# Two weight panels loaded during the second attention, and the first token gather of the expert layer in two parts

## The reference

```python
h = rmsnorm(x, attn_norm)
c_q, c_kv, k_r, q_b, k_b, v_b, gate_a, gate_b = split(h @ w_in)
o_a = mla_attention(c_q, c_kv, k_r, q_norm, w_uq, kv_norm, w_ukv, cos_mla, sin_mla)
o_b = moba_attention(q_b, k_b, v_b, cos_moba, sin_moba)
mixed = sigmoid(gate_a) * (o_a @ w_o_mla) + sigmoid(gate_b) * (o_b @ w_o_moba)
x = x + mixed @ w_out
# hierarchical_moe(rmsnorm(x, ffn_norm)):
#   a group of 8 experts by argmax, then the top 2 of the group by softmax;
#   for each expert e and its tokens xb:
#       y = (silu(xb @ w_g[e]) * (xb @ w_u[e])) @ w_d[e]      # 1024 -> 256 -> 1024
#   and the weighted y are added to x
return rmsnorm(x, final_norm)
```

## Time and profile before

| | |
|---|---|
| median of three runs | 698.22 us (697.89 to 699.25) |
| the profiled execution | 697.33 us, of which the span of the trace is 695.5 us |
| mean granted TensorE clock | 0.988 of full speed |
| PE busy | 653.9 us (94%) |
| DVE / ACT / POOL busy | 334.8 / 327.0 / 378.6 us |
| read from HBM | 179.73 MB, 260 GB/s over the span |

### The profile page before, as it was taken

One profiled execution on the slowest core, in us unless ns is written; L12 is line 12 of the kernel. 1 busy time (PEld: TensorE's weight loads), 2 busy tenths in 40 slices (PEclk: granted clock), 3 DMA queues, 4 the chain that ended last, 5 costly groups with the idle time before them and its releaser, 6 DMA issues.

```text
span 695.5 us, 13827 instructions
## 1 busy us (share of the span) xinstructions
PE 653.9 (94%) x5608; PEld 544.4 (78%) x5608; DVE 334.8 (48%) x684; ACT 327.0 (47%) x603; POOL 378.6 (54%) x284
## 2 busy tenths in 40 slices
PE   5999999999999999999999999999999999787894
PEld 4899899999999999998898999999654554343442
DVE  5869723787871247885764654342521221111102
ACT  6566777866553456665358765442311111011004
POOL 3989557798887989998697655783000000000000
PEclk9999999999999999999999999999999999999998
DMA  8875334445356555474457433799999999999994
GB/s 344 322 291 187 122 122 130 175 127 176 122 165 208 184 184 184 168 249 175 128 176 257 150 128 131 306 422 399 369 419 419 419 420 417 421 420 420 421 416 155
DMA packets 27282, 181.72 MB, mean 261 GB/s; under 512 B 3024, under 2 KB 3280, under 8 KB 6864
## 3 DMA queue, kind: packets, MB, share of 16 engines
q1 hardware_dynamic: 26784, 179.74, 67.8%
q10 hardware_dynamic: 432, 1.05, 0.4%
HBM read 179.73 MB, written 1.05 MB: 260 GB/s over the span
## 4 chain that ended last, share of the span: by engine, by line
PE 83%; DMA 10%; DVE 2%; ACT 2%; issue 1%; POOL 0%; SPq 0%; ACTq 0%; DVEq 0%
PE D L520 49%; PE L L1001 7%; DMA spare<-w_expert_dram 4%; DMA big<-w_expert_dram 4%; PE L L976 3%; PE QB L1049 3%; PE L L704 2%; PE D L568 2%; DMA ring<-w_dense_dram 2%; PE TB L713 2%; PE D L1084 2%; PE TB L1084 1%; PE L L1010 1%; PE L L676 1%; PE D L572 1%; PE D L551 1%
## 5 line engine op out<-in xcount | busy, mean ns | idle before, releaser
L1587 POOL TENSOR_TENSOR ring_r<-ring,ring_r 128x512 fp32r<-128x512 f32 (+1 forms) x280 | 378.4, 1387 | 96.2 <-ACT ring_r L1173 95.8
L520 PE MATMUL D<-scr_r,ring_r 128*128 128x256 f32 x1104 | 209.4, 286 | 0.0
L1173 ACT ACTIVATE ring_r<-ring 128x1024 fp32r<-128x1024 f32 (+2 forms) x140 | 145.1, 1042 | 91.3 <-PE D L520 81.0
L520 PEld LDWEIGHTS D<-scr_r,ring_r 128*128 128x128 f32 x1104 | 172.0, 188 | 2.4 <-issue 1.6
L520 PE MATMUL D<-hT_r,ring_r 128*128 128x256 f32 x552 | 154.0, 279 | 0.0
L520 PE MATMUL D<-big_r,ring_r 128*128 128x256 f32 x1086 | 134.1, 283 | 1.7 <-POOL ring_r L1587 1.7
L520 PEld LDWEIGHTS D<-big_r,ring_r 128*128 128x128 f32 x1086 | 131.3, 188 | 3.4 <-POOL ring_r L1587 2.1
L520 PEld LDWEIGHTS D<-hT_r,ring_r 128*128 128x128 f32 x552 | 103.9, 188 | 1.1 <-issue 0.7
L1604 DVE SCALAR_TENSOR_TENSOR th<-th,L 64x256 f32<-64x256 f32 x32 | 13.4, 418 | 124.5 <-ACT th L1509 123.9
L1509 ACT ACTIVATE th<-L 64x256 f32<-64x256 f32 x16 | 6.0, 377 | 81.1 <-PE L L1001 81.1
L976 PEld LDWEIGHTS L<-wkr,big 128*128 128x128 f32 x240 | 27.9, 191 | 10.6 <-issue 10.6
(11 more groups left out here) (401 smaller groups left out, 1008.2 us busy)
## 6 DMA issues: line engine op xcount, KB each, us to landing
ring<-w_dense_dram SPq DMA_DIRECT2D x69, 1024.0 KB, 4.9
big<-w_expert_dram SPq DMA_DIRECT2D x32, 1024.0 KB, 25.5
ring<-w_expert_dram SPq DMA_DIRECT2D x20, 1024.0 KB, 26.4
spare<-w_expert_dram SPq DMA_DIRECT2D x8, 1024.0 KB, 16.7
wu<-w_expert_dram SPq DMA_DIRECT2D x5, 1024.0 KB, 21.9
small<-w_expert_dram SPq DMA_DIRECT2D x4, 1024.0 KB, 18.6
scr<-w_expert_dram SPq DMA_DIRECT2D x4, 1024.0 KB, 18.5
hT<-w_expert_dram SPq DMA_DIRECT2D x4, 1024.0 KB, 19.4
```

The lines of the kernel that those rows point to most:

```text
L520: last = mm(out_, r32(w[i][ws]), r32(x[j][xs_]), start=start and m == 0, stop=stop and m == 2)
L1173: A_(r32(hi_unit(j)[w]), dense_unit(j)[w], ACT.Copy).then_inc(hi_ready, 1)
L1587: last = g.tensor_tensor(r32(w), w, r32(h).bitcast(F32), ALU.subtract)
```

## The change

There are three edits.

1. The rounded halves of the two attention outputs (`ob_hi`, `oa_hi`) move from `big` 0 to 2K into `small` 2K to 4K, and those of the mixed output (`m2_hi`) from `big` 2K to 4K into `hT`. So `big` 0 to 2K is dead once the keys of MLA are made (unit 107) and `big` 2K to 4K once the last MoBA head is scored. In the list of places they become 5 and 6, `scr` becomes 7, and `hT` goes to place 21.
2. SP loads panel 5 when unit 107 is done and panel 6 when the MoBA scores are made (`logits`), between the laps of dense panels; one panel instead of two is loaded at unit 124, and two instead of three go out together at unit 132 and after. Which load waits for what is otherwise kept.
3. The first group's gather: chunks 0, 1 into bank L0 and 2, 3 into bank QB, with a semaphore step after each, before the branch; DVE stages them in two parts. Gate and up of pair 0 starts when the first part is staged, and waits for the second before its third step. Chunks 4, 5 (bank OB) and 6, 7 (bank L0) are both gathered after its first half, and the second half waits for them in the same way. The other waits are renumbered.

```diff
-        ob_hi, oa_hi = at(big, 0, 4, T), at(big, K, 4, T)
-        m2_hi = at(big, 2 * K, 8, T)
+        ob_hi, oa_hi = at(small, 2 * K, 4, T), at(small, 3 * K, 4, T)
+        m2_hi = hT
...
-        wide_ring = [spare[:, 0, :], spare[:, 1, :], wu[:], small[:, 0:2 * K], big[:, 16 * K + 512:18 * K + 512], scr.rearrange("p c t -> p (c t)"), hT.rearrange("p c t -> p (c t)"),
+        wide_ring = [spare[:, 0, :], spare[:, 1, :], wu[:], small[:, 0:2 * K], big[:, 16 * K + 512:18 * K + 512], big[:, 0:2 * K], big[:, 2 * K:4 * K], scr.rearrange("p c t -> p (c t)"),
...
-            dense_laps(lap_rotated, laps)
+            sp_.wait_ge(unit_done, UNIT0["ukvk"] + 1)
+            expert(5)
+            dense_laps(lap_rotated, lap_rotated + 1)
+            sp_.wait_ge(logits, H1 + 8)
+            expert(6)
+            dense_laps(lap_rotated + 1, laps)
...
             sp_.wait_ge(unit_done, UNIT0["omoba"])
-            expert(5)
-            expert(6)
+            expert(7)
             dense(left.pop(0))
             dense(left.pop(0))
             sp_.wait_ge(o_mm, H1 + 2 * H2)
-            expert(7)
             expert(8)
             expert(9)
-            dense(left.pop(0))
             expert(10)
             dense(left.pop(0))
+            expert(11)
+            dense(left.pop(0))
 
             sp_.wait_ge(unit_done, UNIT0["out2"])
-            expert(11)
             expert(12)
...
+            def gather_first():
+
+                pe.wait_ge(picked, 1)
+                gather_chunks(X, 0, 0, 2).then_inc(gathered, 1)
+                gather_chunks(DN, 0, 2, 2).then_inc(gathered, 1)
...
                 for k in range(4):
-                    if k == 2 and h and p == 0 and counted:
-                        pe.wait_ge(xe_ready, 3)
+                    if k == 2 and p == 0 and counted:
+                        pe.wait_ge(xe_ready, 4 if h else 2)
...
             def gate_up(p):
-                if p == 0:
-                    pe.wait_ge(picked, 1)
-                    gather_chunks(DN, 0, 4, 2).then_inc(gathered, 1)
-                pe.wait_ge(xe_ready, 2 * (p // 2) + (3 if p else 1))
+                pe.wait_ge(xe_ready, 2 * (p // 2) + (4 if p else 1))
...
                 gate_up_half(p, 0, x)
                 if p == 0:
-                    gather_chunks(M, 0, 6, 2).then_inc(gathered, 1)
-                    pe.wait_ge(xe_ready, 2)
+                    pe.wait_ge(picked, 1)
+                    gather_chunks(M, 0, 4, 2).then_inc(gathered, 1)
+                    gather_chunks(X, 0, 6, 2).then_inc(gathered, 1)
+                    pe.wait_ge(xe_ready, 3)
...
-            gather(0, 0)
+            gather_first()
...
-            stage(0, 0)
+            for c0, bank in ((0, X), (2, QB)):
+                dve.wait_ge(gathered, 1 + c0 // 2)
+                stage_chunks(bank, 0, 0, c0, 2).then_inc(xe_ready, 1)
...
-                for c0, bank in ((0, QB), (2, OB)):
-                    dve.wait_ge(gathered, 2 + c0 // 2)
+                for c0, bank in ((0, OB), (2, X)):
+                    dve.wait_ge(gathered, 3 + c0 // 2)
```

More of the change, by code:

```diff
@@ L247, in build @@
         sel = wkr.rearrange("p c n -> p (c n)").rearrange("p (a b c) -> p a b c", a=2, b=NT)
-        wide_ring = [spare[:, 0, :], spare[:, 1, :], wu[:], small[:, 0:2 * K], big[:, 16 * K + 512:18 * K + 512], scr.rearrange("p c t -> p (c t)"), hT.rearrange("p c t -> p (c t)"),
+        wide_ring = [spare[:, 0, :], spare[:, 1, :], wu[:], small[:, 0:2 * K], big[:, 16 * K + 512:18 * K + 512], big[:, 0:2 * K], big[:, 2 * K:4 * K], scr.rearrange("p c t -> p (c t)"),
                      attn[:, 0:2 * UNIT], cst[:, CST["center"]:CST["center"] + 2 * K],
-                     big[:, 4 * K:6 * K], big[:, 6 * K:8 * K], big[:, 0:2 * K],
+                     big[:, 4 * K:6 * K], big[:, 6 * K:8 * K],
                      big[:, 14 * K:16 * K], big[:, 12 * K:14 * K], ring[:, 2, :], ring[:, 3, :], ring[:, 0, :],
-                     ring[:, 4, :], ring[:, 1, :], ring[:, 5, :], big[:, 10 * K:12 * K], big[:, 2 * K:4 * K],
+                     ring[:, 4, :], ring[:, 1, :], ring[:, 5, :], big[:, 10 * K:12 * K], hT.rearrange("p c t -> p (c t)"),
                      xT.rearrange("p c t -> p (c t)")]
@@ L969, in gather @@
                 if g:
-                    pe.wait_ge(xe_ready, 2 * g + half + 1)
+                    pe.wait_ge(xe_ready, 2 * g + half + 2)
                 gather_chunks(X, g, 4 * half, 4).then_inc(gathered, 1)
+            def gather_first():
+                pe.wait_ge(picked, 1)
+                gather_chunks(X, 0, 0, 2).then_inc(gathered, 1)
+                gather_chunks(DN, 0, 2, 2).then_inc(gathered, 1)
             def gather_chunks(into, g, c0, n):
@@ L1136, in _ @@
                         last.then_inc(swt_mm, 1)
-                        pe.wait_ge(xe_ready, w + 1)
+                        pe.wait_ge(xe_ready, w + 2)
                         gate_up_half(p, 0, lambda c, e: xe[:, c, e * WIN:(e + 1) * WIN], counted=False)
@@ L2032, in picks @@
                 if g >= 2:
-                    dve.wait_ge(gathered, 2 * g - 1)
+                    dve.wait_ge(gathered, 2 * g)
                 pick(sel[:, g % 2], slice(4 * g, 4 * g + 4)).then_inc(picked, 1)
@@ L2064, in stage @@
             def stage(g, half):
-                dve.wait_ge(gathered, 2 * g + half + (2 if g else 1))
-                if g:
-                    dve.wait_ge(gu_done, 2 * g - 2 + half)
+                dve.wait_ge(gathered, 2 * g + half + 3)
+                dve.wait_ge(gu_done, 2 * g - 2 + half)
                 stage_chunks(X, g, half, 0, 4).then_inc(xe_ready, 1)
@@ L2129, in _ @@
             with dve.Else():
-                dve.wait_ge(xe_ready, 1)
+                dve.wait_ge(xe_ready, 2)
                 weights(0)
@@ L2138, in _ @@
                         weigh(0, sel[:, 0, :, 0:2 * WIN], p).then_inc(weighted, 1)
-                        dve.wait_ge(gathered, w + 1)
+                        dve.wait_ge(gathered, w + 2)
                         staged(xe, X[:, :].rearrange("p (a b) -> p a b", a=DC), 0, DC).then_inc(xe_ready, 1)
```

## The result

The changed kernel took 704.78 us, the median of four runs (701.87 to 705.78), against 698.74 us for the kernel before (697.89 to 699.27): a ratio of 1.0081, 95% interval 1.0048 to 1.0114. It is slower, and 704.78 lies outside the predicted range. Twelve more runs of the same kernel, in a later set beside 29 of the kernel before, gave 701.48 (699.03 to 705.26) against 699.08 (697.21 to 705.84), ratio 1.0017 [0.9986, 1.0047].

A forecast was written before the change was run, and what follows sets the result against it. PE was taken to bound the kernel up to the gather, then the expert stream and a fixed tail. Loads 0, stall +0.7 and gather -0.95 sum to -0.25 us: 698.0 against the median 698.22, no change; range 695.9 to 699.7.

The forecast's parts named there:

- What bounds the kernel: Whole kernel: PE until it frees places for panels 23 and 24, then 1.7 us, 73 panels at 419 GB/s, fixed tail.
- Loads as a gain, 0: Expert stream: loading panels 5 and 6 earlier gains 0, since panel 23 still waits for PE to free a place.
- the hole grow from 2 us to 4: DMA before the stream's restart: backlog ends 2.5 us earlier, so windows from 493 to 497 us are emptier.
- 56 lands one panel later: 2.5 us: Second attention: panel 5 goes ahead of dense panel 56, which lands 2.5 us later; bounds 0 and 5.0 us.
- A shift of 2.5 us leaves a stall of 0.7 us on PE: PE's transposes near 377 us: ACT's rounding of panel 56 shifts 2.5 us, leaving PE a 0.7 us stall.
- Slack 1.8 us: Second attention: ACT's copy of transposed probabilities ends at 374.96, 1.8 us before PE needs its bank at 376.77.
- The second rival: Second attention: panels 5, 56, 57 share the rate, 56 is 5.0 us late, PE stalls 3.2; sum +2.25, 700.5 us; 8%.
- The gather, -0.95 us: Expert layer's start: gate and up starts earlier, freeing panels 23 and 24 at 495.05 instead of 496.00; gain 0.95 us.
- the cover: Stream's restart: panels 25 and 26, issued at 499.2, flow from 500.9, before two panels finish at 501.75; margin 0.85 us.
- Panel 6, the new homes of the halves, the branch: Loads before dense panel 60, moved rounded halves, and gate and up behind the branch: each forecast to cost 0.
- the third rival: Gate and up behind the branch: a gap of 1.04 us on PE undoes the gather's gain; sum +0.8, 699.0 us; 12%.
- The range: Whole kernel's time: 695.9 to 699.7 us.

The follow-up runs named there:

- f2_both_early: Kernel before plus the two-part first gather, with three of the four products gathering chunks 6 and 7 left out; 699.23 us, ratio 1.0004.
- e4_busy_wait: Changed kernel plus 16 useless PE products ahead of the transposes for which PE waits in the second attention; 704.71 us, ratio 1.0107.
- f1_second_early: Kernel before, with three of the four products that gather chunks 6 and 7 of the first group left out; 698.87 us, ratio 0.9997.
- e1_gather_only: Kernel before with only the two-part first gather added; loads, places and rounded halves as before; 699.46 us, ratio 1.0005.
- e2_loads_only: Kernel before with only the new places, moved rounded halves and early panels 5 and 6, old gather (the loads alone); 702.46 us, ratio 1.0063.
- e8_halves_old_loads: Kernel before plus the two-part first gather, with expert panels 23 to 26 loaded in halves; 699.82 us, ratio 1.0005.
- e6_busy_wait_short: Changed kernel plus 4 useless PE products ahead of the transposes for which PE waits in the second attention; 701.10 us, ratio 1.0035.

## Why the prediction was wrong, point by point

- **What bounds the kernel: right.** PE up to the gather, then the stream, then a fixed tail. A delay of PE at the gather reached the last landing in every row of the table.
- **Loads as a gain, 0: right, with a wrong picture.** I had the backlog end 2.5 us earlier and the hole grow from 2 us to 4. In the changed kernel the rate stays at 360 GB/s or more until 499 us, and the first hole is two or three microseconds wide as before. The early panels thinned slices 28 and 29; the backlog's last panels go out when PE frees their places, so its end did not move against PE (near 499.2, 3.6 us later than before, with PE 3.3 late ahead of the low clock near 489 us).
- **"56 lands one panel later: 2.5 us": the step that failed first.** It was 3.8 us: panel 5 landed 4.0 us behind panel 4, not 2.5, and 56 2.3 behind it. The step took the mean rate for a transfer's time. The rows had the counterexample, which I had not worked out: panel 57 landed 4.0 us behind 56 in the kernel before.
- **"A shift of 2.5 us leaves a stall of 0.7 us on PE": mis-sized.** Slack 1.8 us was right: 3.82 - 1.8 = 2.0, and 1.93 was measured. The sum held, its first term did not.
- **The missing term: the clock.** The sum priced PE's idle time at its length. The clock at 1.2 GHz behind it cost 1.6 us more in both profiles of the changed kernel, so 1.93 became 3.6. No rival had it. A kernel with a longer wait at this place (the loads alone, 3.1 us) did not pay it, so it is a cost that may come, not one that must.
- **The second rival was the nearest.** It named the place, and a stall of 3.2 us from both loads sharing the rate; its 2.25 us stands beside the 2.4 of the larger sample. It got 8%, on the order of landings alone. Its threshold (rounding later than 376.3) was not reached, and the loss came from a smaller delay and the clock.
- **The gather, -0.95 us: the issue right, the gain not.** 23 and 24 went out 0.92 us earlier as forecast, and the last landing did not. The step that failed is the cover ("499.2 + 1.7 = 500.9 is before that. The cover is 0.85 us") or what it leaves out. Where the loads are whole, a hole of 0.6 to 1.0 us at full rate does open in six of seven profiles, 2 to 4 us behind the issue of 25, which the cover denied. But with that hole closed (`f2_both_early`) the last landing came no earlier either, so that the hole took the gain is not shown, and the cause stays open.
- **Panel 6, the new homes of the halves, the branch: no cost, as forecast.** PE is even 0.25 us faster between 384 and 476 us, where the prediction has 0. It shows no gap behind the branch (QB products at 496.65, gate and up at 497.64), so the third rival fell.
- **The range.** 704.78 is 6.0 us above the kernel before, and 2.4 to 3.4 are the change's own. The rest probably is events that runs of the kernel before have too: the one profiled run of the four, 701.87 us, has a second low clock of 1.3 us near 489 us, and the other three were not profiled. A range that took the spread of the three runs shown (1.4 us) for that of the kernel was too narrow: 35 runs of the kernel before reach from 696.93 to 705.47.

The best versions, with panel 5 behind dense panel 56, are equal to the kernel before within 1.3 to 2 us, not faster.

## What to carry to other kernels

Before a bulk load is put ahead of a small queue of loads that someone waits for, look for the one with no slack: here moving the same transfer behind one dense panel removed the loss. Read how long the second and third transfer of a burst took, not the mean rate. Price a new wait of PE with what the clock may do behind it. And don't count an earlier issue as an earlier landing: here 0.9 us of the one brought nothing of the other.

## What the runs showed of the hardware

- **A low clock that comes without a wait.** Nine of the fourteen profiles have 1.2 GHz between 489 and 493 us (486 to 489 where nothing delayed PE before, 492 to 495 in `e4_busy_wait`), among the router's small products, with PE busy ahead of it. `f1_second_early`, which up to there is the kernel before, has it, and the second profile of the changed kernel has not:

```profile
487.00:488.00 1.00, 1.00 (x6) 1.00 (x6) 0.88 (x8) 0.00 (x0) 0.00 (x0) 0.50 0.98 303
```
```profile
489.00:490.00 1.00, 1.00 (x10) 1.00 (x10) 0.39 (x3) 0.26 (x1) 0.00 (x0) 1.00 0.87 324
```

  It costs 1.3 us on PE, and the runs of the kernel before lie in groups near 697.5 us (mean clock 0.988) and 698.8 (0.986), which fits a run without it and one with it.
- **A subtraction of DVE that takes nine times as long.** The rests of four chunks, 128x512 each, are made beside GpSimd's own subtractions. First `e1_gather_only`, where one is slow, then the first of the four in the second profile of the kernel before, where none is:

```profile
293.76 12.43 DVE L1628 TENSOR_TENSOR hT_r<-hT,scr_r 128x512 fp32r<-128x512 f32 x4 [0.31 <-ACT scr_r L1187]
```
```profile
293.61 0.93 DVE L1623 TENSOR_TENSOR hT_r<-hT,scr_r 128x512 fp32r<-128x512 f32 x1 [0.32 <-ACT scr_r L1182]
```

  One of the four took 8.44 us instead of 0.93; PE then is 3.6 us late at 302 us. It came in three of fourteen profiles at this place (in a fourth, the second one of the changed kernel, the first subtraction took 3.45 us and PE lost nothing), with the same program in front, and why is open. `e2_loads_only` has the like at 27 us: its four subtractions take 12.23 us instead of 6.83, the clock is at 0.50 from 39.3 to 42.7, and PE is 5.4 us late from there on.
- **Here transfers in halves restarted slower.** Four transfers of 0.5 MB and four more behind them brought 111 to 213 GB/s in 499 to 502 us, where whole panels reached 400 two to three microseconds behind their issue. Whether the end suffers from it is not shown: against PE the last landing is 0.9 us later in this kernel, 0.0 in `e8_halves_old_loads` with the same halves, and 0.9 in `e6_busy_wait_short` with whole panels.
